# A two-block model in one program: GpSimd splits weights with a wait after every instruction, the row mask moves from VectorE to ScalarE, the bank counter restarts per layer, and key-doubling products use 64 rows each

## The reference

```python
def first_block(x, ...):
    for l in range(2):
        h = rmsnorm(x, attn_norm[l])
        (q, kc, vc, ksl, vsl, kwn, vwn, gts, gq, gk, gv, ga, gr, uv) = split_columns(h @ w_in[l])
        o_nsa = nsa_mixer(q, kc, vc, ksl, vsl, kwn, vwn, gts, ...)   # 8 query heads, 2 key groups
        o_gla = gla_mixer(gq, gk, gv, ga, gr, ...)                   # 4 heads, decay per channel
        o_sg = spatial_gating(uv, ...)
        x = x + concatenate([o_nsa, o_gla, o_sg]) @ w_out[l]
        h = rmsnorm(x, ffn_norm[l])
        x = x + (silu(h @ w_gate[l]) * (h @ w_up[l])) @ w_down[l]
    return rmsnorm(x, final_norm)

def second_block(x, c, ...):
    h = rms_norm(x, g_pre) * (1 + scl) + shift
    xa, za, q, k, v, zb, ga, gb = split(h @ w_in_2)
    y_a = (forward + backward linear recurrence of conv(xa)) * silu(za) @ w_pa
    y_b = neighbourhood_attention(q, k, v, rpb) * silu(zb) @ w_pb
    x = x + gate * ((sigmoid(ga) * y_a + sigmoid(gb) * y_b) @ w_o)
    return rms_norm(x, g_final)
```

## Time and profile before

| | |
|---|---|
| median of 3 runs | 2050.62 us (2049.79 to 2055.84) |
| the profiled execution's own time | 2054.61 us |
| its span, first to last instruction | 2052.6 us |
| busy: PE, DVE, ACT, POOL | 1924.2, 1160.2, 615.6, 1419.6 us |
| granted TensorE clock, mean over the span | 0.969 of full |

### The profile page before, as it was taken

The page is one execution under the profiler, slowest core; times in us unless marked ns, Lnnn a source line. Parts: engine busy times, 40 slices in busy tenths (PEclk is TensorE's granted clock), DMA queues, the critical chain, the costliest instruction groups (busy, mean ns, idle before and its releaser), DMA issues.

```text
span 2052.6 us, 28491 instructions
## 1 busy us (share of the span) xinstructions
PE 1924.2 (94%) x10022; PEld 1489.2 (73%) x10022; DVE 1160.2 (57%) x1670; ACT 615.6 (30%) x1116; POOL 1419.6 (69%) x1208
## 2 busy tenths in 40 slices
PE   7898889999999999988899999997999999989997
PEld 5676557888888877755588888885777777768775
DVE  5765774466257347478556704654937666650353
ACT  4124662210011131266531100113036566540111
POOL 8554117988789985511298978886897878757772
PEclk9999989999999999999999999998999999999998
DMA  5132002343334222300124433542132233222221
GB/s 204 53 96 80 22 11 83 122 143 108 97 121 136 92 72 81 116 21 22 32 93 123 133 100 96 148 124 67 51 108 84 79 94 87 76 72 93 84 91 41
DMA packets 68680, 182.44 MB, mean 89 GB/s; under 512 B 23888, under 2 KB 24144, under 8 KB 68432
## 3 DMA queue, kind: packets, MB, share of 16 engines
q1 hardware_dynamic: 60480, 154.48, 24.8%
q10 hardware_dynamic: 8080, 26.32, 4.1%
HBM read 178.67 MB, written 2.10 MB: 88 GB/s over the span
## 4 chain that ended last, share of the span: by engine, by line
PE 70%; DVE 13%; ACT 7%; issue 6%; POOL 2%; DMA 1%; ACTq 0%; DVEq 0%; POOLq 0%
PE PS L402 21%; PE PS L406 20%; PE PS L405 20%; POOL w_lo L2083 2%; PE PS L691 1%; PE PS L653 1%; PE PS L641 1%; PE PS L441 1%; ACT P L1251 1%; ACT rg L1322 1%; DVE gN L1472 1%; DVE P L1946 1%; PE PS L538 1%; POOL w_hi L2079 1%; DVE PS L1620 1%
## 5 line engine op out<-in xcount | busy, mean ns | idle before, releaser
L2079 POOL TENSOR_TENSOR w_hi<-raw,const 128x256 fp32r<-128x256 f32 (+1 forms) x602 | 641.9, 1088 | 586.1 <-PE PS L402 578.2
L2083 POOL TENSOR_TENSOR w_lo<-raw,w_hi 128x256 fp32r<-128x256 f32 (+1 forms) x602 | 783.9, 1324 | 13.4
L402 PE MATMUL PS<-a_hi,w_hi 128*128 128x512 f32 x1616 | 651.7, 403 | 42.3 <-POOL w_lo L2083 14.1
L405 PE MATMUL PS<-a_lo,w_hi 128*128 128x512 f32 x1616 | 635.8, 393 | 0.0
L406 PE MATMUL PS<-a_hi,w_lo 128*128 128x512 f32 x1616 | 635.3, 393 | 0.0
L402 PEld LDWEIGHTS PS<-a_hi,w_hi 128*128 128x128 f32 x1616 | 307.1, 190 | 128.6 <-issue 46.0
L406 PEld LDWEIGHTS PS<-a_hi,w_lo 128*128 128x128 f32 x1616 | 307.2, 190 | 65.9
L405 PEld LDWEIGHTS PS<-a_lo,w_hi 128*128 128x128 f32 x1616 | 307.6, 190 | 64.8 <-issue 3.4
L1793 DVE TENSOR_TENSOR work<-PS,rstd 128x512 f32<-128x512 f32 x88 | 60.8, 691 | 147.6 <-PE PS L406 140.9
L402 PE MATMUL PS<-f_hi,w_hi 128*128 128x512 f32 x352 | 138.7, 394 | 0.0
L406 PE MATMUL PS<-f_hi,w_lo 128*128 128x512 f32 x352 | 138.0, 392 | 0.0
(11 more groups left out here) (290 smaller groups left out, 2494.1 us busy)
## 6 DMA issues: line engine op xcount, KB each, us to landing
raw<-weights SPq DMA_DIRECT2D x278, 512.0 KB, 3.5
work<-mod_w ACTq DMA_DIRECT2D x24, 512.0 KB, 3.6
work<-cmp_w ACTq DMA_DIRECT2D x8, 1024.0 KB, 5.6
bias<-rpb SPq DMA_DIRECT2D x256, 12.0 KB
rgw<-rgw ACTq DMA_DIRECT2D x8, 256.0 KB, 2.6
out<-xc SPq DMA_DIRECT2D x8, 256.0 KB, 2.0
const<-const SPq DMA_DIRECT2D x1, 1436.5 KB, 15.3
x<-x_t SPq DMA_DIRECT2D x4, 256.0 KB, 6.8
```

Of the source, the lines that this page charges most:

```text
L402: ins = nc.tensor.matmul(out, wh, hi, start=start, stop=False)
L405: nc.tensor.matmul(out, wh, lo, start=False, stop=False)
L2079: G.tensor_tensor(w_hi[:, r, k, :], raw[:, r, k, :], ones[:, k, :], ALU.mult).then_inc(pool_chain, 1)
L2083: ins = G.tensor_tensor(w_lo[:, r, k, :], raw[:, r, k, :], w_hi[:, r, k, :].bitcast(F32), ALU.subtract)
```

## The change

Four edits.

1. **The split.** `split(n, hi_parts, lo_parts)` multiplies by the number 1.0 with a tensor_scalar, which reads `raw` alone, in 2 parts of 4 tiles. Behind each part come its parts of `w_lo`. GpSimd waits for the end of every instruction before it issues the next. There are 4 parts of `w_lo` in the slots listed by `fine_slot` and 2 elsewhere. `fine_slot` lists "in", the first two "out" of a layer, and "in2" up to 6*KT, each by itself and not by the ring's turn, without slot 0. The hardware loops are gone: the 282 slots are written out.
2. **The row mask.** The product of `gN` and `rowok` becomes a ScalarE Copy with a scale per partition, between the sigmoid and L1009. VectorE's L1472 is gone.
3. **The bank counter.** `pool_of["next"]` is set to 0 at the start of each layer.
4. **The doubling products.** `spread` gives `dup` and `rotdup` only the 64 rows of the key group, and the matching 64 rows of `proj`, so that the products of the two groups lie in different halves of the rows. For `ksl` and `kwn` the order changes from dup 0, rot 0, dup 1, rot 1 to dup 0, dup 1, rot 0, rot 1.

```diff
             for l in range(DEPTH):
-                pool_of["banks"] = 4
+                pool_of["banks"], pool_of["next"] = 4, 0
+                def spread(key, matrix, g, t):
+                    r = slice(HD * g, HD * g + HD)
+                    one(key, c_(matrix)[r, g * P:(g + 1) * P], proj[r, t, :])
...
                     elif name in ("ksl", "kwn"):
                         pe.wait_ge(*emptying((l, name)))
-                        for g in range(GROUPS):
-                            one((l, name, "dup", g), c_("dup")[:, g * P:(g + 1) * P], proj[:, t, :])
-                            one((l, name, "rot", g), c_("rotdup")[:, g * P:(g + 1) * P], proj[:, t, :])
+                        for what, matrix in (("dup", "dup"), ("rot", "rotdup")):
+                            for g in range(GROUPS):
+                                spread((l, name, what, g), matrix, g, t)
...
+                        act.wait_ge(act_chain.sem, act_chain.raised())
+                        if l == 0:
+                            act.wait_ge(const_in, 16)
+                        A(gN[:, 0, 2:24:3], gN[:, 0, 2:24:3], ACT.Copy, scale=c_("rowok"))\
...
-                        g = gN[:, 0, 2:24:3]
-                        TS(g, g, c_("rowok"), None, ALU.mult).then_inc(dve_chain.sem, 1)
-                        dve.wait_ge(dve_chain.sem, dve_chain.raised())
...
+            def split(n, hi_parts, lo_parts):
+                r = n % RING
+                pool.wait_ge(raw_in[r], 16 * (n // RING + 1))
+                if n >= RING:
+                    pool.wait_ge(slot_used, n - RING + 1)
+                each, per = 8 // hi_parts, lo_parts // hi_parts
+                for h in range(hi_parts):
+                    k = slice(h * each, (h + 1) * each)
+                    G.tensor_scalar(w_hi[:, r, k, :], raw[:, r, k, :], 1.0, None, ALU.mult).then_inc(pool_chain, 1)
+                    spent[0] += 1
+                    pool.wait_ge(pool_chain, spent[0])
+                    for q in range(h * per, (h + 1) * per):
+                        k = slice(q * 8 // lo_parts, (q + 1) * 8 // lo_parts)
+                        ins = G.tensor_tensor(w_lo[:, r, k, :], raw[:, r, k, :], w_hi[:, r, k, :].bitcast(F32), ALU.subtract)
+                        if q < lo_parts - 1:
+                            ins.then_inc(pool_chain, 1)
+                            spent[0] += 1
+                            pool.wait_ge(pool_chain, spent[0])
+                ins.then_inc(split_done, 1)
+            def fine_slot(n):
+                item = PLAN[n]
+                return item[0] == "in" or item[0] == "out" and item[2] < 2 or item[0] == "in2" and item[1] < 6 * KT
             pool.wait_ge(head_in, 16)
+            for n in range(SLOTS):
+                if n and fine_slot(n):
+                    split(n, 2, 4)
+                else:
+                    split(n, 2, 2)
```

More of the change, by code:

```diff
@@ L102 @@
              + [(m, k) for m in range(OUT_EARLY, KT) for k in range(KT)])
-PIECES = 4
-def beside_vector(item):
-    if item[0] == "in2":
-        return item[1] < 6 * KT
-    return item[0] == "in" or item[0] == "gate" and item[2] < 2
 def stream_plan():
@@ L452, in further @@
                         for g in range(GROUPS):
[L453 removed]
+                            spread((l, name, "dup", g), "dup", g, t)
                     elif name in ("ksl", "kwn"):
                         pe.wait_ge(*emptying((l, name)))
[L456 to L458 removed]
+                        for what, matrix in (("dup", "dup"), ("rot", "rotdup")):
+                            for g in range(GROUPS):
+                                spread((l, name, what, g), matrix, g, t)
                     elif name[0] == "q":
@@ L2067, in _ @@
             G = nc.gpsimd
-            ones = c_("ones")[:, 0:1].unsqueeze(2).to_broadcast([P, 8, P])
-            def split(r, arrival, used, chain, pieces):
-                pool.wait_ge(raw_in[r], arrival)
-                if used is not None:
-                    pool.wait_ge(slot_used, used)
-                each = 8 // pieces
-                for n in range(pieces):
-                    k = slice(n * each, (n + 1) * each)
-                    G.tensor_tensor(w_hi[:, r, k, :], raw[:, r, k, :], ones[:, k, :], ALU.mult).then_inc(pool_chain, 1)
-                for n in range(pieces):
-                    k = slice(n * each, (n + 1) * each)
-                    pool.wait_ge(pool_chain, chain + n + 1)
-                    ins = G.tensor_tensor(w_lo[:, r, k, :], raw[:, r, k, :], w_hi[:, r, k, :].bitcast(F32), ALU.subtract)
+            spent = [0]
@@ L2084, in split @@
                 ins.then_inc(split_done, 1)
-            def pieces_of(turn):
-                return PIECES if any(beside_vector(item) for item in PLAN[turn * RING:(turn + 1) * RING]) else 1
+            def fine_slot(n):
+                item = PLAN[n]
+                return item[0] == "in" or item[0] == "out" and item[2] < 2 or item[0] == "in2" and item[1] < 6 * KT
             pool.wait_ge(head_in, 16)
-            turns = SLOTS // RING
-            first, chain = 0, 0
-            while first <= turns:
-                n = pieces_of(first)
-                last = first + 1
-                while 1 <= first and last < turns and pieces_of(last) == n:
-                    last += 1
-                if 1 <= first < turns and last - first > 1:
-                    with pool.Fori(first, last) as i:
-                        for r in range(RING):
-                            split(r, i * 16 + 16, i * RING + (r - RING + 1),
-                                  i * (RING * n) + (chain + (r - RING * first) * n), n)
-                    chain += (last - first) * RING * n
-                else:
-                    last = first + 1
-                    for r in range(RING if first < turns else SLOTS % RING):
-                        split(r, 16 * (first + 1), first * RING + r - RING + 1 if first else None, chain, n)
-                        chain += n
-                first = last
```

2 lines of the change are left out of this document (1 added, 1 removed).

## The result

The changed kernel takes 2081.56 us (median of 4 runs, 2081.04 to 2082.41); the kernel before, on the same chip, 2052.77. The ratio is 1.0141, 95% interval 1.0122 to 1.0159: **1.4% slower**, where 1.6% faster was forecast. The profiled execution took 2081.67 us, its span is 2079.5. It is rival (d) that came true.

What follows compares the result with a forecast made beforehand. TensorE, busy 94% of the span, was taken as the bound. Terms -11.4 - 7.4 - 8.3 - 3.2 - 0.5 - 2.5 = -33.3 from 2054.6 gave 2021.3; the median, 4.0 lower, was forecast at 2017 us, range 2005 to 2034.

Steps and rivals of the forecast that it cites:

- rival (d): GpSimd becomes the bound in feed-forward parts and output stage: +67, 2084 us at a one-input price of 2.65; chance 0.05.
- the term for GpSimd's own time: Split slots: one-input w_hi 1.3 us for 8 tiles, slot about 4.5 us, covered by TensorE's 5.48.
- The mask and the waits: Layer 0, z to first doubling product: without mask and with pauses it runs as layer 1; -11.4 us in sum.
- My lower bound: For the mask and pauses in layer 0: only -1 us if another VectorE instruction is shut out instead.
- The bank counter: Layer 1's gk takes free bank 1, without waiting for VectorE or half clock behind it; -7.4 us.
- The doubling products: Pairs of 64-row products in both layers save 0.74 us each; -8.3 us, bounds -4 and -10.3.
- odd wait: Among the doubling products, VectorE can follow TensorE with only an occasional wait; the term stays at -8.3 us.
- half is lost to VectorE: Bound of the doubling products' term: -4 us.
- Rival (b): VectorE paces the doubling products, half their gain goes, shorter shut-outs give nothing: 2024 us; chance 0.10.
- The starved round: First round of the second block's attention should cost what the next does; -3.2 us, bounds -3.6 and 0.
- Shorter shut-outs elsewhere: VectorE's y_lo and like places: a quarter of 10 us comes back; -2.5 us, bounds +3 and -7.

Runs made afterwards that it cites:

- experiments 7: The change's tensor_scalar in the pieces and order of the kernel before, without waits between pieces; the other three edits kept; 2018.46 us.
- 8: The change with coarse slots split in one part instead of two, fine slots as changed; 2029.65 us.
- experiment 1: The change with only w_hi put back to the two-input product with ones, waits and parts kept; 2044.71 us.
- experiments 3: The kernel before with only the row mask moved to ScalarE; 2056.64 us, ratio 1.0008.
- 12: The change with w_hi by copy, waits kept, and the row mask back on VectorE; 2015.85 us.
- 13: The change with w_hi by copy, pieces and order of before without waits, and the row mask back on VectorE; 2011.54 us.
- experiment 14: The kernel before with only w_hi made by copy, its loops written out; 2022.40 us.
- experiments 2: The change with the whole GpSimd split of before, the other three edits kept; 2044.52 us.
- experiments 4: The change with w_hi by tensor_copy in place of tensor_scalar, waits and parts kept; 2015.39 us.
- 10: The change with w_hi by copy, and key-doubling products over all 128 rows again, in the new order; 2022.53 us.

## Why the prediction was wrong

**The step that failed** is the term for GpSimd's own time, and in it two prices. "Its price lies between 0.95 us ... and 1.89 or somewhat above for 8 tiles; I take 1.3, since the nearest row reads twice as much." It measured 2.98 in halves and 2.77 whole: outside the bounds that I had called bounds. No row showed the instruction, and I reasoned from the number of inputs. The four forms show that this number does not order the prices: one input 0.71 us as a copy, 1.57 as a tensor_scalar, two inputs 1.15. The second price, 0.15 us for each extra instruction and 0.08 for each gap, together 0.46 a slot, was better: 0.57 measured with tensor_scalar (5.80 - 5.23), of which 0.37 are the waits.

"The slot is then about 4.5 us. ... Covered everywhere by 5.48 of TensorE" fell with it. Cover is a threshold: 5.23 costs nothing, 5.43 costs 18 us over the two parts, 5.80 costs 52. The dear form alone is covered in the feed-forward parts (experiments 7 and 8), the halves with their waits alone too (experiment 1, 4.86). Only together they are over. What the prediction named as the sign of (d), TensorE waiting for `w_lo` in the feed-forward part, is what the profile shows. Rival (d) had the mechanism, the threshold ("over 0.34 us more than the 1.89") and the time for a price of 2.65; it got 0.05 because "it reads half as much". With a price that no row shows and a margin of 0.34 us on a term repeated in 132 slots, that chance was far too low.

**The mask and the waits**, -11.4. The segment fell by 11.8 us in layer 0, so the size was right, and it rose by 1.1 in layer 1, where GpSimd was late. The reason was half wrong: the mask's move earns 0 alone and 0 beside copies with or without waits (experiments 3, 12, 13). What ends the shut-out is the waits (35.1 us with the two-input product, experiment 1, though no run has that with the mask on VectorE) or the cheaper `w_hi` (35.7 us with the copy alone, experiment 14). My lower bound, "another VectorE instruction is shut out in its place", is what happens with the split of before (experiments 2 and 3). ScalarE's extra instruction did its part as forecast, 0.31 us.

**The bank counter**, -7.4: 6.2 in the change, 7.2 and 7.8 where GpSimd keeps up. Right.

**The doubling products**, -8.3. TensorE's saving per four products was right (1.56 us, two times 0.74 forecast), the "odd wait" was mis-sized: 3 to 7 us remain with copies and waits (4.5 by the segments of experiments 4 and 10), near the bound I gave for "half is lost to VectorE", and by the segments nothing without waits (experiments 13 and 14). In the change itself only 1.4 and -0.5 us show. Rival (b) was right for this term.

**The starved round**, -3.2: 3.6. Right.

**Shorter shut-outs elsewhere**, -2.5. Too small: from the last round to the last norm the change gains 7.5 us although its slots are longer, and the kernel with copies 12.3. VectorE is busy 98.1 us of that stretch before, 74.2 in the change and 73.6 with copies and waits; in the row of eight `y_lo` products I had counted on, 12.68 became 9.28 in the change. Over the whole span VectorE went from 1160.2 to 1001.0 us busy.

**That the copy kernel lands at 2015, where I forecast 2017 for the change, is partly chance**: the pairs gave some 4 us less and the last stage some 10 more than I had put down.

## What to carry to other kernels

Price an instruction by its form from a row, or from a short run that measures it, before a stream of hundreds rests on it; the number of operands says little. Where an engine feeds another with a margin, as GpSimd feeds TensorE here, add up everything that the change puts on its slot (form, cuts, waits) and compare with the margin first: below it costs are free, above it each is multiplied by the number of slots. And to end a shut-out, shorten or break the run of the engine that causes it; here, moving the one instruction that showed it only handed it to the next.

## What the runs showed of the hardware that was not expected

- GpSimd makes float32r out of float32, 4 tiles of 128 columns, in 0.61 us as a copy, 1.04 as a product with a tile of ones, 1.49 as a tensor_scalar with either a multiplication or an addition.
- Waiting for the end of each of a slot's four GpSimd instructions costs 0.37 us together (5.80 against 5.43), cutting two into four 0.20 (5.43 against 5.23).
- A VectorE instruction can be held over many GpSimd instructions that follow each other without a gap, and not only over one: 16.55, 14.91, 12.3 us until the run's end for whichever instruction came to stand there, and 4.54 where the run was shorter. But it is not always held to the end: 5.17 us with GpSimd running on for another 4.6 (experiment 14), and 5.23 us with 8.3 more in the kernel before. A run in which every other group is a tensor_scalar let it in after 0.81 us. What decides is open: in all of these the `w_lo` products between are the same.
- Beside tensor_scalar VectorE's product at L1796 takes 0.70 us (mean of 44, the change); beside the product with ones, with the same waits, 1.13 (experiment 1).
